# A second stream of work beside expert gathers: the beats of the context spread anew, and a new choice of the up vectors that VectorE adds

## The reference, cut to what matters

```python
def peer_ffn(x, w_query, sub_keys, expert_down, expert_up):
    ...
        top_s, sel = lax.top_k(cand, PEER_TOPK)
        eidx = jnp.take_along_axis(cidx, sel, axis=-1)
        g = jax.nn.softmax(top_s, axis=-1)
        u = expert_down[eidx]
        vv = expert_up[eidx]
        act = jax.nn.gelu(jnp.einsum('td,thkd->thk', xc, u).astype(jnp.float32), approximate=False)
        return jnp.einsum('thk,thkd->td', (g * act).astype(x.dtype), vv)
```

```python
    for l in range(DEPTH):
        last = l == DEPTH - 1
        ...
        if last:
            kc, vc = kv_heads(hn @ w_in[l][:, OFF_K:OFF_F], k_norm_g[l])
        else:
            pc = hn @ w_in[l]
            qc = q_heads(pc[..., OFF_Q:OFF_K], q_norm_g[l])
            kc, vc = kv_heads(pc[..., OFF_K:OFF_F], k_norm_g[l])
        ...
        if not last:
            attn_c = attend(qc, kc, vc)
            h = mixers_and_ffn(h, pc, attn_c, mod_c[2], mod_c[3], mod_c[4], mod_c[5], g_norm2[l],
        ...
```

## Time and profile before

| | us |
|---|---|
| median of 3 runs | 3145.93 |
| lowest and highest | 3140.52, 3148.44 |
| the profiled execution | 3139.5 |
| its span, first to last instruction | 3137.6 |
| TensorE busy | 2681.7 (85%) |
| VectorE busy | 1604.0 (51%) |
| GpSimd busy | 999.6 (32%) |
| ScalarE busy | 602.4 (19%) |
| moved by DMA | 817.45 MB, mean 261 GB/s |

### The profile page before, as it was taken

One profiled execution on the slowest core, in us unless ns is written; L12 is line 12 of the kernel. 1 busy time (PEld: TensorE's weight loads), 2 busy tenths in 40 slices (PEclk: granted clock), 3 DMA queues, 4 the chain that ended last, 5 costly groups with the idle time before them and its releaser, 6 DMA issues.

```text
span 3137.6 us, 28943 instructions
## 1 busy us (share of the span) xinstructions
PE 2681.7 (85%) x9764; PEld 1788.0 (57%) x9764; DVE 1604.0 (51%) x3671; ACT 602.4 (19%) x1272; POOL 999.6 (32%) x1040
## 2 busy tenths in 40 slices
PE   7898977987879788998779998967676899977999
PEld 6466733533435355677336665733254788845888
DVE  1531467988877525314788777678626100044100
ACT  2241112322120012411123331021022200122100
POOL 0000366665666610002566664566700000000000
PEclk9899999999989998999889999988886899967999
DMA  6445699998999954456899999999920344411344
GB/s 249 148 161 215 251 376 367 409 383 328 373 363 404 410 215 147 152 194 265 320 361 411 412 411 364 379 383 364 396 81 14 107 149 159 147 41 67 134 157 152
DMA packets 187291, 817.45 MB, mean 261 GB/s; under 512 B 20592, under 2 KB 22656, under 8 KB 154128
## 3 DMA queue, kind: packets, MB, share of 16 engines
q0 software_dynamic: 148784, 549.31, 45.4%
q1 hardware_dynamic: 38368, 266.35, 23.2%
HBM read 814.54 MB, written 1.05 MB: 260 GB/s over the span
## 4 chain that ended last, share of the span: by engine, by line
PE 53%; DVE 17%; POOL 10%; issue 9%; DMA 5%; another core or an unknown queue 4%; ACT 1%; DVEq 0%; ACTq 0%; SPq 0%; POOLq 0%
PE work L589 45%; PE acc L589 7%; DVE arena L1615 6%; POOL arena L547 5%; POOL arena L572 5%; DMA arena<-experts_down,arena 3%; DVE arena L1464 2%; DMA ring<-stream 1%; DVE arena L1644 1%; PE work L663 1%; DVE arena L1568 1%; DVE arena L1569 0%; DVE arena L1571 0%; DVE arena L1570 0%
## 5 line engine op out<-in xcount | busy, mean ns | idle before, releaser
L589 PE MATMUL acc<-arena 128*128 128x512 f32 x1824 | 914.5, 650 | 269.6 <-issue 155.3
L589 PE MATMUL work<-arena,ring 128*128 128x256 f32 x3460 | 767.9, 384 | 32.2 <-ACT arena L1395 14.5
L589 PEld LDWEIGHTS acc<-arena 128*128 128x128 f32 x1824 | 365.6, 207 | 747.5 <-issue 588.5
L572 POOL DMA_INDIRECT arena<-experts_down,arena x512 | 495.5, 968 | 851.3 <-DVE arena L1599 662.3
L589 PEld LDWEIGHTS work<-arena,ring 128*128 128x128 f32 x3460 | 666.5, 193 | 138.2 <-issue 26.3
L1615 DVE SCALAR_TENSOR_TENSOR arena<-arena,acc 128x1024 f32<-128x1024 f32 x512 | 610.2, 1217 | 161.5 <-DMA arena<-experts_down,arena 85.5
L547 POOL DMA_INDIRECT arena<-experts_up,arena x512 | 496.9, 971 | 400.3 <-PE acc L589 148.9
L589 PE MATMUL work<-h,ring 128*128 128x256 f32 x1440 | 338.0, 394 | 11.1 <-issue 9.8
L589 PEld LDWEIGHTS work<-h,ring 128*128 128x128 f32 x1440 | 281.2, 198 | 66.5 <-issue 27.3
L589 PE MATMUL work<-lent,ring 128*128 128x256 f32 x992 | 224.3, 379 | 0.0
L589 PEld LDWEIGHTS work<-lent,ring 128*128 128x128 f32 x992 | 188.5, 190 | 52.5 <-issue 30.1
(11 more groups left out here) (230 smaller groups left out, 1651.0 us busy)
## 6 DMA issues: line engine op xcount, KB each, us to landing
ring<-stream SPq DMA_DIRECT2D x252, 1024.0 KB
arena<-experts_down,arena POOLq DMA_INDIRECT x512
arena<-experts_up,arena POOLq DMA_INDIRECT x512
arena<-na_bias POOLq DMA_DIRECT2D x2, 2048.0 KB, 15.0
arena<-consts POOLq DMA_DIRECT2D x1, 2392.0 KB
lent<-consts POOLq DMA_DIRECT2D x2, 1024.0 KB
arena<-consts POOLq DMA_DIRECT2D x1, 1816.0 KB
x<-x_in SPq DMA_DIRECT2D x1, 1024.0 KB, 5.7
```

The lines of the kernel that those rows point to most:

```text
L572: pool.indirect_dma_start(down[:, (l * PICKS + n) % ROWS, :], None, experts[2 * l], bass.IndirectOffsetOnAxis(ap=expert[:, n:n + 1], axis=0))\
L589: ins = nc.tensor.matmul(o, w, r, start=start, stop=stop, **kw)
```

## The change

Every beat of the context gets a new place. Layer 0 starts at group 8, layer 1 at group 4, and the parts of a chain on different engines stand further from each other. In layer 1 the feed-forward takes two of three beats and the keys come at the end. Three score buffers instead of two, two for the transposed scores instead of one, one root buffer for each of three head groups instead of one, and a square buffer for each, so some waits for their reuse go. The up vectors that VectorE adds are now the last pick of every other group beside `cffn` and of every group beside `cffo`, 47 in all, and none elsewhere. GpSimd's loads move from pick 16 to 20 and from 240 to 248. TensorE runs what is left of the context's beats before its second tile's end. No arithmetic of the reference changes.

```diff
-SIDE = 4
+Y_AT = 4
 DIAGS = 8
-SIDE_AT = 16
+CONTEXT_AT = (8, 4)
+FFN_AT, FFO_AT = 14, 84
 def beside(l, n):
-    return l == 1 and n % SLOTS >= SIDE_AT and n % SIDE == SIDE - 1
+    q, last = divmod(n, GROUP)
+    beat = q - CONTEXT_AT[1]
+    if l == 0 or last != GROUP - 1 or q % TILE_GROUPS < 2 * Y_AT:
+        return False
+    return FFO_AT <= beat < FFO_AT + 2 * KD or FFN_AT <= beat < FFO_AT and q % 2 == 1
+def last_beside(l, t):
+    return max(n for n in range(t * SLOTS, (t + 1) * SLOTS) if beside(l, n))
...
-CONTEXT_AT = 12
...
-        put(1, "cnorm")
+        put(2, "cnorm")
         for i in range(N_FM2):
-            put(10 + 2 * i, "cfm")
+            put(14 + 2 * i, "cfm")
...
         for u in range(CONTEXT_UNITS):
-            put(32 + 3 * u, "cS")
-            put(38 + 3 * u, "cT")
-            put(40 + 3 * u, "cO")
-        for beat, name in ((60, "cmean"), (62, "cdft"), (63, "cdft"), (66, "cdft"), (67, "cpool"), (68, "cpool"),
-                           (69, "cfour"), (70, "cfour"), (71, "cplin"), (72, "cplin"), (73, "cvar"),
-                           (79, "cpw"), (80, "cpw")):
+            put(38 + 3 * u, "cS")
+            put(47 + 3 * u, "cT")
+            put(51 + 3 * u, "cO")
+        for beat, name in ((61, "cmean"), (64, "cdft"), (67, "cdft"), (70, "cpool"), (73, "cdft"), (74, "cpool"),
+                           (77, "cfour"), (78, "cfour"), (79, "cplin"), (80, "cplin"), (81, "cvar"),
+                           (89, "cpw"), (90, "cpw")):
             put(beat, name)
         for n in range(KD):
-            put(83 + 2 * n, "cout")
+            put(94 + 2 * n, "cout")
     else:
-        put(1, "cfnorm")
-        for j in range(2 * KF):
-            put(10 + j, "cffn")
+        put(2, "cfnorm")
+        for j in range(KF):
+            put(FFN_AT + 3 * j, "cffn")
+            put(FFN_AT + 3 * j + 1, "cffn")
         for n in range(KD):
-            put(57 + 2 * n, "cffo")
-        for beat, name in ((78, "cknorm"), (87, "ckey"), (89, "cval"), (90, "ckn")):
+            put(FFO_AT + 2 * n, "cffo")
+        for beat, name in ((107, "cknorm"), (116, "ckey"), (117, "cval"), (120, "ckn")):
             put(beat, name)
...
-                    if n == TOPK:
+                    if n == TOPK + ROWS // 2:
...
-                    if n == PICKS - TOPK:
+                    if n == PICKS - ROWS:
...
+                    if t:
+                        for _ in context:
+                            pass
                     if l:
                         add_side(t)
...
-                        elif beat == 3:
+                        elif beat == 5:
                             root_c(rnorm_f, "cnorm")
...
-                        elif beat == 4:
+                        elif beat == 7:
                             inverse_c(rnorm_f, "cnorm")
...
-                        elif beat == 77:
+                        elif beat == 105:
                             copied(act, "cffo", KD - 1)
                             squares_c("sqk_c")
-                        elif beat == 80:
+                        elif beat == 110:
                             root_c(rnorm_f, "cknorm")
...
-                        elif beat == 93:
+                        elif beat == 123:
                             inverse_c(key_rs_c, "ckn")
                             V.step(stt(key_c[:, 1, :], key_raw_c, k2("g_k", 1, c2_v), key_rs_c), "qk_normed_c")
```

More of the change, by code:

```diff
@@ L218, in item_table @@
         context = context_items(l)
-        for q in range(CONTEXT_AT, GROUPS):
+        for q in range(CONTEXT_AT[l], GROUPS):
             if q == TILE_GROUPS + Y_AT // GROUP:
                 add(f"ytr{l}", 2)
-            for name in context.get(q - CONTEXT_AT, ()):
+            for name in context.get(q - CONTEXT_AT[l], ()):
                 add(name)
@@ L1217, in _, with shift_c @@
                 score(PEER_HEADS - 1)
-                def shift_c(beat, scaled, done, layer, chunk):
-                    for k in (2 * beat, 2 * beat + 1):
+                def shift_c(ks, scaled, done, layer, chunk):
+                    for k in ks:
                         A.need(scaled, k + 1)
@@ L1231, in root_c, with turned @@
                     A.free(f(o, b[:, 0:T], ACT.Sqrt, bias=k1("eps")), item, j)
+                def turned(u):
+                    b = A.full("cT", u)
+                    A.free(f(prob_t_c[u % 2], b[:, 0:T], ACT.Copy), "cT", u)
                 def context_mixers():
-                    for beat in range(83):
-                        i, odd = divmod(beat - 12, 2)
-                        unit, phase = divmod(beat - 32, 3)
+                    for beat in range(94):
+                        i, odd = divmod(beat - 17, 2)
+                        unit, phase = divmod(beat - 38, 3)
                         if beat == 0:
@@ L1623, in add_beside @@
                     V.need(f"up_full{m % ROWS}", 16 * (m // ROWS + 1))
-                    if j == SIDE_AT + SIDE - 1:
+                    if not any(beside(l, m) for m in range(t * SLOTS, n)):
                         if t:
@@ L1686, in context_mixers @@
                     taps = convolve_c()
-                    for beat in range(86 + 2 * KD):
-                        unit, phase = divmod(beat - 32, 3)
-                        if beat == 2:
+                    for beat in range(98 + 2 * KD):
+                        unit, phase = divmod(beat - 38, 3)
+                        if beat == 6:
                             V.need("c2_c_loaded", 16)
@@ L1716, in context_mixers @@
+                            V.step(v.tensor_reduce(mx[:, s, 0:1], prob_c[s], AX.X, ALU.max))
                             V.step(v.tensor_scalar(neg_mx[:, s, 0:1], mx[:, s, 0:1], -1.0, None, ALU.mult), "score_c")
-                        elif 37 <= beat < 62 and phase == 2 and unit <= CONTEXT_UNITS:
-                            u = unit - 1
-                            s = u % 2
+                        elif 46 <= beat < 70 and phase == 2:
+                            u = unit - 2
+                            s = u % 3
```

282 lines of the change are left out of this document (139 added, 143 removed).

## The result

| | before | changed |
|---|---|---|
| median, us | 3145.93 | 3120.05 |
| lowest and highest of 5 | 3140.52, 3151.69 | 3107.16, 3121.66 |
| span of the profiled execution | 3137.6 | 3113.9 |
| layer 0's expert phase (first to last dots) | 749.7 | 751.7 |
| layer 1's expert phase | 801.5 | 772.5 |

The changed kernel takes 0.9909 of the time before, 95% interval 0.9884 to 0.9934: 26 us less, where 37 were forecast. The two phases tell more than the sum. Layer 1 gave 29 us, more than the 22.5 that its parts had (2.5 of the start, 6, 7, 9, less 2); layer 0 gave nothing in these two executions, where 14.5 were expected (2.5, 4, 8); what lies outside the phases is 3 us longer in this execution.

A forecast was written before the change was run, and what follows sets the result against it. It took the expert phases to be bound by DMA at 412 GB/s, with 131 us lost below that rate. Terms 5+4+0+0+8+6+7+9-2+0 = 37 us took 3139.5 to 3102.5, as a median 3109, range 3082 to 3143.

The forecast's parts named there:

- Full rate as the measure of loss: Both expert phases: time with DMA below 412 GB/s counts as lost, 131 us in all, the ceiling of savings.
- 1, the loads later: Starts of both layers: loads at pick 20, not 16, end GpSimd's score wait; 5 us, bounds 0 to 7.1.
- 2 and 5, layer 0's distances: Layer 0, 420 to 558 and 797 to 933 us: wider beats and more buffers save 4 and 8 us.
- The second rival: Both phases: lost time is VectorE's own work and the tile change, not the context's; 3139, no change; chance 0.12.
- 3 and 4: Layer 0, 558 to 757 us, with the same VectorE instructions, and both layers' change of token tile: 0 each.
- 6, groups 8 to 31 of layer 1: Layer 1, 1528 to 1649 us: root's wait goes and side picks leave VectorE; 6 us, bounds 0 to 13.8.
- 7 and 8, beside cffo and after it: Layer 1: TensorE relieved beside cffo, groups at DMA's 6.84 us, saves 7; afterwards twelve side picks leave VectorE, 9.
- 9, the keys at the end: Layer 1's last groups: the context's keys, together with the later load of constants, cost 2 us, bounds 0 to 4.
- 10, the spread of the feed-forward: Layer 1: feed-forward on two of three beats, DMA 17.8 us per three groups against TensorE's 15.0; gains nothing.
- The clock: Layer 1 beside the feed-forward: TensorE's clock falls, at 0.70 costing 84 us, total 3193; chance 0.08.
- The waits come back: Both phases: results seen two groups late leave about half the distance gains, 19 or 20 us, near 3127; chance 0.22.
- the signs named: Waits under 3 us, two stretches above 385 GB/s, cffo groups 6.9 us, clock over 0.9; wrong if over 115 us lost.

The follow-up runs named there:

- e6: Kernel before with only the new rule for VectorE's up vectors (34 of them), on the second kind of chip: ratio 0.9990.
- e5: Kernel before with only cffn spread over two of three beats, cffo and all behind it 19 beats later: ratio 0.9947.
- e10: Changed kernel with up rows fetched four picks behind the down rows instead of two, first kind of chip: ratio 0.9853, 3101.3 us.
- e4: Changed kernel with up rows fetched four picks behind the down rows instead of two, second kind of chip: ratio 0.9938.

## Why the prediction was right, and where not

The time, 3120, lies in the range, the direction is right, the size is 26 of 37 us. That it came this near is in part luck: some 11 us of the sum were not there in layer 0, and the spread, which the sum had at nothing, gave more than was forecast in layer 1. The steps:

- **Full rate as the measure of loss** held: none of these stretches is above 412 GB/s in any run, and layer 1's gain of 29 us shows as 30 us of lost time that went.
- **1, the loads later: 5 us.** Measured 2.1 and 2.9 in the starts. The feared wait of ScalarE for xc did come, 3.43 us; the start gained in spite of it, so the cover held at least in the main.
- **2 and 5, layer 0's distances: 4 and 8 us.** This is the step that failed. Groups 8 to 31 got 1.1, groups 72 to 103 lost 2.3 more, and over all traces of the first kind layer 0 is some 3 us shorter, the start included. I had taken half the lost time of the stretch because waits of the context stood in it; the waits were there, but the loss was not theirs. In groups 72 to 103 the old distances lose 1.2 us in a job without late signals (e6), and the new ones 18 to 20 us in those with them. The second rival, that the lost time is not the context's, had this right for layer 0 and was given 0.12.
- **3 and 4:** 0, and they came out at -2.8 and, over both layers, +1.8.
- **6, groups 8 to 31 of layer 1: 6 us.** 4.2.
- **7 and 8, beside cffo and after it: 7 and 9 us;** 9, the keys at the end: 2 lost. Together 14 expected, 22 measured. Part 7's mechanism is shown: the side rule takes 8 to 12 us from TensorE's way through cffo. Its floor of 6.84 us a group was wrong: the 16 groups beside cffo took 103 us, 6.44 each, at 408 GB/s, so 42.0 MB moved in them and not 45.1, and the rest of their weights came outside of them.
- **10, the spread of the feed-forward, costed at nothing.** That was the largest error in one term: alone it is worth 16.5 us (e5). I had only asked whether TensorE and the clock would bear it, and not what it does for the groups that get the weights. The 22 us above are the side rule's and the spread's together. A move takes work from one stretch and gives it to another, and both have to be costed.
- **The clock** stayed at 0.96 in groups 32 to 63 (1.00 before), with TensorE busy 181 of 207 us, and at 0.95 in groups 72 to 87. That rival did not come. The Trainium skill (TensorE: Matmul & The Clock Gate, HAM oscillation) speaks of an array that is clocked down again after each wait. The prediction's estimate for that in every group was 284 us, where the phase got 29 shorter; the trace agrees with it only in that the mean fell by some hundredths. The prediction misread one row beside it: among the sparser stretches the lowest is 0.84 and not 0.85.
- **The waits come back** (first rival, 3127): no. The reciprocals, and GpSimd at the two loads, wait no more. Its own terms, 5 + 2 + 3 + 2 + 7 + 4 - 2, add up to 21 and not 19 or 20, so about 3125; and the upper bounds of the parts add up to 75, not 70. The measured time lies inside the range either way. At 3120 the total can't tell this rival from the forecast; the single waits and layer 1 do.

Of the signs named, these came: the reciprocals' waits and GpSimd's for the score gone, cffo's groups at 6.4 us and 408 GB/s, the clock over 0.9 beside the feed-forward (but for the change of token tile, 0.87 there, 0.88 before), and lost time of 103 us, under the 115 that would have made it wrong. Groups 8 to 31 of layer 1 came to 383 GB/s, just short of 385. These did not come: layer 0's groups 72 to 103 above 385 (365 and 369 GB/s), its groups 32 to 63 at 388 (383), and a root that waits under 3 us in layer 0 (4.01).

What stays open: what makes signals late in one job and not in another, whether the missing records of those traces have the same cause, and whether it is the lateness or something beside it that costs layer 0 its 45 us; why the spread is worth 16.5 us, as TensorE's relief beside cffo is at most 5 of them; and what the change alone is worth on the second kind, where it was not run. Of its two halves only the side rule was: 0.9990 there.

## What to carry to other kernels

Cost a stretch by what its binding queue loses, and then ask of each wait in it whether taking it away moves that loss; a wait that ends last on its own engine may still cost the phase nothing. Work that brings transfers of its own may also be cover: the reading that fits most rows here, not shown by a run of its own, is that spread evenly it gives each group time to make up for a late signal, and packed it leaves stretches in which nothing can be made up. Two edits that relieve the same stretch are to be tried one by one, as the larger may be the one that was costed at nothing.

## What the hardware showed that was not expected

The same kernel differs by 2.3 to 2.7% between jobs (3139 to 3151 against 3068 us, and one job of each kind has the chip number 5), though DMA's full rate is 409 to 412 GB/s in both and an issue on GpSimd takes 1.24 us in both. Most of the difference lies in the expert phases (layer 0: 748.6 against 710.1 us, layer 1: 769.5 against 759.9, of 57 us in all, e10 and e4). It goes with signals between engines that are seen two and more microseconds late, and with traces that lack half of the signals' records, in the jobs of the one kind only. The worth of an edit depends on it: the side rule is 0.9938 on one and 0.9990 on the other.
